# Order of the out products of the last two weight slabs of four two-stream layers (context first, latents after)

## What is computed

```python
def ffn_sublayer(x, shift, scale, gate, w_in, w_out, ln_g, ln_b):
    y = swiglu_2(modulate_2(x, shift, scale), w_in, w_out)
    return layer_norm(ALPHA * x + 0.5 * gate * y, ln_g, ln_b)
```

## Time and profile before

| | |
|---|---|
| median of 3 runs (lowest, highest) | 2701.93 us (2701.62, 2702.2) |
| the profiled execution, its time | 2698.95 us |
| its span, first to last instruction | 2697.1 us |
| its mean granted TensorE clock | 0.971 |
| TensorE matmul busy | 2531.8 us, 94% |
| VectorE busy | 1851.8 us, 69% |
| ScalarE busy | 1101.2 us, 41% |
| read from memory | 448.99 MB |

### The profile page before, as it was taken

One profiled execution on the slowest core, in us unless ns is written; L12 is line 12 of the kernel. 1 busy time (PEld: TensorE's weight loads), 2 busy tenths in 40 slices (PEclk: granted clock), 3 DMA queues, 4 the chain that ended last, 5 costly groups with the idle time before them and its releaser, 6 DMA issues.

```text
span 2697.1 us, 39723 instructions
## 1 busy us (share of the span) xinstructions
PE 2531.8 (94%) x15724; PEld 2282.1 (85%) x15724; DVE 1851.8 (69%) x3539; ACT 1101.2 (41%) x1631; POOL 0.2 (0%) x4
## 2 busy tenths in 40 slices
PE   4999989889989999899999899999899999798997
PEld 4998889789988888688888898888898888777997
DVE  7878977788879965535555569886584444575665
ACT  3444555344453323634222652222642222545443
POOL 0000000000000000000000000000000000000000
PEclk8999999989989999999999999999999999898999
DMA  8876846768767742422222266665273332312552
GB/s 310 299 247 201 269 160 232 263 228 288 246 197 251 221 138 68 146 94 86 86 91 90 86 189 206 191 196 195 87 269 122 94 101 76 92 57 74 186 185 96
DMA packets 161097, 452.65 MB, mean 168 GB/s; under 512 B 17680, under 2 KB 21264, under 8 KB 160912
## 3 DMA queue, kind: packets, MB, share of 16 engines
q1 hardware_dynamic: 160912, 450.11, 51.2%
HBM read 448.99 MB, written 1.05 MB: 167 GB/s over the span
## 4 chain that ended last, share of the span: by engine, by line
PE 58%; DVE 6%; ACT 4%; issue 1%; DMA 0%; SPq 0%; ACTq 0%; DVEq 0%
PE PS L985 18%; PE PS L986 18%; PE PS L987 18%; DVE wlo L1445 2%; ACT whi L1189 1%; PE PS L1006 1%; PE PS L1008 1%; DVE X L1534 1%; PE PS L1124 1%; DVE X L1532 1%; ACT NT L1242 1%; DVE RS L1501 1%; PE PS L1170 0%; DVE Ul L1538 0%; PE PS L1153 0%
## 5 line engine op out<-in xcount | busy, mean ns | idle before, releaser
L1445 DVE TENSOR_TENSOR wlo<-raw,whi 128x1024 fp32r<-128x1024 f32 x602 | 736.1, 1223 | 490.3 <-ACT whi L1189 487.6
L985 PE MATMUL PS<-Uh,wlo 128*128 128x256 f32 (+1 forms) x2992 | 972.8, 325 | 77.4 <-DVE Ul L1538 42.0
L986 PE MATMUL PS<-Ul,whi 128*128 128x256 f32 (+1 forms) x2992 | 954.3, 319 | 0.0
L987 PE MATMUL PS<-Uh,whi 128*128 128x256 f32 (+1 forms) x2992 | 954.2, 319 | 0.0
L1189 ACT ACTIVATE whi<-raw 128x1024 fp32r<-128x1024 f32 x602 | 632.7, 1055 | 718.7 <-PE PS L987 716.9
L985 PEld LDWEIGHTS PS<-Uh,wlo 128*128 128x128 f32 x2992 | 580.9, 194 | 131.3 <-issue 44.9
L986 PEld LDWEIGHTS PS<-Ul,whi 128*128 128x128 f32 x2992 | 583.5, 195 | 35.0 <-issue 0.2
L987 PEld LDWEIGHTS PS<-Uh,whi 128*128 128x128 f32 x2992 | 582.6, 195 | 34.9
L985 PE MATMUL PS<-Hh,wlo 128*128 128x256 f32 (+1 forms) x1616 | 529.5, 328 | 9.9 <-DVE X L1428 4.1
L986 PE MATMUL PS<-Hl,whi 128*128 128x256 f32 (+1 forms) x1616 | 514.1, 318 | 0.0
L987 PE MATMUL PS<-Hh,whi 128*128 128x256 f32 (+1 forms) x1616 | 513.9, 318 | 0.0
(11 more groups left out here) (170 smaller groups left out, 1918.9 us busy)
## 6 DMA issues: line engine op xcount, KB each, us to landing
MODS<-in_mm SPq DMA_DIRECT2D x168, 256.0 KB, 3.7
SCR<-in_mm SPq DMA_DIRECT2D x168, 256.0 KB, 3.7
raw<-in_f0i SPq DMA_DIRECT2D x64, 512.0 KB, 3.8
raw<-in_f1i SPq DMA_DIRECT2D x56, 512.0 KB, 3.5
raw<-in_f2i SPq DMA_DIRECT2D x56, 512.0 KB, 3.6
SCR<-in_ma SPq DMA_DIRECT2D x88, 256.0 KB, 5.0
raw<-in_w1i SPq DMA_DIRECT2D x44, 512.0 KB, 4.4
raw<-in_w2i SPq DMA_DIRECT2D x44, 512.0 KB, 4.3
```

The costliest lines, as they stand in the source:

```text
L985: e.matmul(o, ll, rh, start=start, stop=False)
L986: e.matmul(o, lh, rl, start=False, stop=False)
L987: return e.matmul(o, lh, rh, start=False, stop=stop)
L1445: e.tensor_tensor(wlo[:, w.n % RING, :], raw[:, w.n % RING, :], whi[:, w.n % RING, :].bitcast(F32), ALU.subtract).then_inc(s["wlo"].tell(w ...
```

## The change

The last slab but one of f0, go, f1 and f2 is no longer run for both streams at once. `outer_halves` is given the last two slabs. It runs the last but one for the context alone (by `outer`), then the last one for the context with squares and sums as before. The filler now holds two generators: the last slab's products for the latents, without squares and sums (its four pieces are still in the ring), and after them the last but one slab's products for the latents, now with squares and sums. These call `chunk` again, so the four pieces of that slab are fetched and split a second time, and `outer` got a parameter `every` so that it gives out one product at a time. The filler of the context's norm is thus sixteen products long instead of eight. On VectorE the order of the accumulations on a tile of X is no longer that of the slabs' numbers, so `x_before` now looks up which accumulation on that tile was the last.

```diff
-    def outer(self, st, w_out, first, slab, at, qs, r, norm=None):
+    def outer(self, st, w_out, first, slab, at, qs, r, norm=None, every=0):
...
             if mm % per == per - 1:
                 self.used[c] = (w.id, 0)
+            if every or mm % per == per - 1:
                 yield
...
-    def outer_halves(self, st, w_out, first, slab, at, qs, norm):
-        per, n0 = 8 // len(slab), len(self.stream)
-
-        def half(r):
+    def outer_halves(self, st, w_out, last_two, norm):
+        (first0, slab0, at0, qs0), (first, slab, at, qs) = last_two
+        per = 8 // len(slab)
+        self.drain(self.outer(st, w_out, first0, slab0, at0, qs0, CTX))
+        n0 = len(self.stream)
+
+        def kept(r):
             for mm in range(KT):
...
-                w = self.out_tile(st, n0 + c, slab, at, qs, mm, r, n0 + c, norm, True)
+                w = self.out_tile(st, n0 + c, slab, at, qs, mm, r, n0 + c, norm, r is CTX)
...
-        self.drain(half(CTX))
-        self.filler.append(half(LAT))
+        self.drain(kept(CTX))
+        self.filler.append(kept(LAT))
+        self.filler.append(self.outer(st, w_out, first0, slab0, at0, qs0, LAT, norm, 1))
...
-            if n:
+            if n and (r is not BOTH or n < len(slabs) - 1):
                 yield from out(n - 1)
...
-            self.outer_halves(st, w_out, firsts[n], slabs[n], n + at, [slots[f] for f in slabs[n]], norm)
+            self.outer_halves(st, w_out, [(firsts[i], slabs[i], i + at, [slots[f] for f in slabs[i]]) for i in (n - 1, n)], norm)
...
-        if n:
+        if 0 < n < len(CSLABS) - 1:
             p.drain(p.outer("go", "go", 4 * (n - 1), CSLABS[n - 1], n - 1, [((n - 1) % 2) * FS + i for i in range(FS)], BOTH))
-    n = len(CSLABS) - 1
-    p.outer_halves("go", "go", 4 * n, CSLABS[n], n, [(n % 2) * FS + i for i in range(FS)], True)
+    p.outer_halves("go", "go", [(4 * n, CSLABS[n], n, [(n % 2) * FS + i for i in range(FS)])
+                                for n in (len(CSLABS) - 2, len(CSLABS) - 1)], True)
...
-            def x_before(st, at, k, h):
-
-                if at and (st, at - 1, k, h) in s["acc"].at:
-                    on.wait_ge(s["acc"], (st, at - 1, k, h))
+            added = {}
+
+            def x_before(st, k, h):
+
+                if (st, k, h) in added:
+                    on.wait_ge(s["acc"], added[st, k, h])
                     return
...
+                    added[st, k, h] = (st, at, k, h)
```

More of the change, by code:

```diff
@@ L1426, in accumulate @@
                     on.wait_ge(s["coef"], (st, h))
-                    x_before(st, at, k, h)
+                    x_before(st, k, h)
                     e.scalar_tensor_tensor(out=X[:, k, l:u], in0=PS[:, bank[0], l:u], scalar=cf((st, h))[:, k:k + 1],
```

## The result

| | before | after |
|---|---|---|
| median (8 runs each, one chip) | 2701.78 us (2699.6 to 2702.84) | 2709.45 us (2707.1 to 2711.2) |
| the profiled execution, its span | 2698.95, 2697.1 us | 2707.65, 2705.9 us |
| mean granted clock | 0.971 | 0.969 |

The ratio is 1.0029 (95% interval 1.0019 to 1.0039): the kernel is slower by 7.7 us, where +9.2 was forecast.

The account below looks back on a forecast made before the run. TensorE, busy for 94% of the span, was taken to bound the kernel. Stage terms of 1.1 + 1.1 + 2.3 + 3.6 and 1.1 for f1's modulation work made +9.2 us on 2701.93, thus 2711, range 2698 to 2720.

Parts of the forecast that it names:

- Parts 1 and 2: Last slab but one as narrow products: 10.3 us less in its context pass, 11.5 more for latents; cost 1.25 per stage.
- Part 3: Sixteen more pieces of weights, four per stage, fetched and split again on ScalarE and VectorE: taken as costing nothing.
- Part 4: During the context's norm, waits for Ul go; TensorE idles 8.6 us for the re-fetched slab's first square, about the same size.
- The second wait of 1.6 us: TensorE waits 1.6 us more, for the square of the re-fetched slab's third latent product, which ends at 1925.3.
- Part 5: After the 8.6 us idle the clock is at 1.2 GHz: 1.0 us more per stage (ends 0 and 1.4).
- Part 6: Stage by stage, clock included: f0 +3.6, go +2.3, f1 and f2 +1.1 each, plus 1.1 for f1's modulation work.
- The clock's term: Low clock behind the long idle in each of the four stages: +1.0 us per stage.
- its first tile starts 0.4 us later after A; so +1.3: In go, the context norm's first tile starts 0.4 us later after the context's last sums: +1.3 us, with the clock +2.3.
- The lag: In f1, VectorE's modulation work falls behind the narrow products: ends 0 and 2.2 us, taken 1.1.
- The stall is really covered: Rival: squares ready when TensorE asks; 11 us less per stage in go, f1 and f2, nothing in f0; about 2669; 12%.
- It moves and costs little: Rival: clock returns at once, f1's VectorE keeps up, f0's latent tiles catch up; +3 us, 2705; 20%.
- The repeated weights come late: Rival: re-fetched pieces 2 to 4 each hold TensorE for a 2.3 us weights pass, 27 us in all, 2739; 8%.

Follow-up runs that it names:

- experiment 1: Kernel before, with the last slab but one as two narrow products per output tile, nothing moved or loaded twice: 2705.53 us, ratio 1.0020.
- experiment 2: Kernel before, with the last slab but one run for the context, then at once for the latents with weights fetched again: 2711.97 us, ratio 1.0041.
- experiment 3: Changed kernel, with two filler products instead of one after each tile of the context's norm: 2698.35 us, ratio 0.9992.
- experiment 5: Changed kernel, with the re-fetched slab's latent sums one product behind instead of two in f0, go and f1: 2714.36 us, ratio 1.0052.
- experiment 6: Changed kernel, with the re-fetched slab's latent sums three products behind instead of two in f0, go and f1: 2706.86 us, ratio 1.0022.
- experiment 11: Changed kernel, with three filler products per tile of the context's norm and f1's modulation work held back: 2694.01 us, ratio 0.9973.
- experiment 4: Changed kernel, with f0 left as in the kernel before: 2706.78 us, ratio 1.0023.

## Why the prediction came out as it did

**Parts 1 and 2 held.** -10.24 before A for -10.3, f1 apart. The cost of the width, 1.25, was measured alone as 1.03 to 1.32 per stage. The estimate from the Trainium skill's smaller figure would have made experiment 1 a change of 1 us; it was 4.9 ahead of A and 4.6 in the medians.

**Part 3 held, but for one stage.** The sixteen pieces cost nothing in f0, go and f2 (experiment 2). In f1 the loading of M beside modulation work isn't free.

**Part 4 held.** Its main figure was right to 0.1 us, for the reason given: the accumulation of M0 is queued behind tile 4's Ul. That it was so exact is luck in part: 1918.0 was got as 1.2 us before the last pair at its old time, while by the same text the pair itself moves to 1918.4. The accumulation starts 0.4 us before a pair, and the pair came where it was forecast (A + 23.7), so the two slips cancel. Experiments 3, 5, 6 and 11 move that wait from 9.97 down to 1.58 us by places in the order alone. The second wait of 1.6 us, for the square of M2, was nearly absent (0.11 us in f1). Work at half clock filled that time, so these two terms overlapped, and A to E came close to the 43.2 us that part 4 has without the clock.

**Part 5 was too large.** The clock was 0.50 for 10.2 us in f0, go and f2 and 6.8 in f1, beginning inside the long idle, as foretold. But its +1.0 per stage, added to part 4's times, was hardly there. The sums of M2 stand in part 4 at 1925.35, or A + 30.65, with the clock at full. They started at A + 30.77 in f0, 30.83 in go, 30.65 in f1 and 31.22 in f2: 0.9 us in all, for 4.0. TensorE in f1, the product that starts at A and the sums of M2:

```profile
1891.38 0.47 PE L993 MATMUL PS<-Hh,wlo 128*128 128x256 f32 x1
...
1922.03 0.70 PE L1014 MATMUL PS<-X,ones 128*128 128x256 f32 x2
```

Work slowed by the clock took the place of the wait of 1.6 us. What the clock would cost without the long wait is open: no experiment had the one without the other.

**Part 6.** The stages came out at 2.8, 0.8, 3.2 and 0.5 us for 3.6, 2.3, 2.2 and 1.1; the errors are -0.8, -1.5, +1.0 and -0.6, together -1.9 of 9.2. The clock's term was 0.4 to 1.0 us too large in each, and explains f0, which was right in sign and rank, and f2. In go a second step failed as well, "its first tile starts 0.4 us later after A; so +1.3": this difference of go from f1 was carried over, and it is gone. Its first tile now starts at A + 7.6 for A + 7.5 in f1, the wait for the square is the same 8.53 us, and A to E takes 43.0 us for 43.4. In f1 the clock's error is hidden by terms that were too small. The lag was forecast 1.1 and measured 2.0, still within the 0 to 2.2 given. The figures per piece were right (3.27 for 3.3), but behind the 0.4 x 4 us a 0.35 us wait already stood, and the cover I assumed for part of it wasn't there. And behind A TensorE has two waits that the prediction lacked, 0.43 us for the square of M4 and 0.4 more for wlo. So the 7.7 us lie nearer to the 9.2 than the single terms do.

**The rivals.** *The stall is really covered* fails with the 8.53 us. Its deciding point was M0's accumulation before 1910, or A + 15.3; it ran at 1914.71, or A + 23.3. But experiment 11 comes near to that case: with 1.58 us left it gains 7 us, not 33. Its price was also too high by its own part 4: 43.2 us less the waits of 8.6 and 1.6 is 33.0 us of work, not 31.5. The rival supposed that all 12 us of idling per stage could be filled; the accumulations and weights passes that come with the products which fill TensorE's time also stretch VectorE's chain behind them. *It moves and costs little* was too low for f1 and f0. *The repeated weights come late* was right nowhere as told, with no wait for wlo in M, but its engine, VectorE, was the one that made f1 late ahead of A.

## What to carry to other kernels

Filling an idle engine with work only helps if what the filler hands on to other in-order queues stands early enough there: look for the filler's own accumulations and squares in those queues, and work out where they start, before counting the idle time as won. A pass split in two has a price per instruction that the trace already shows, to be set against it (here 13 ns per pair, 5 us in all). And when work is added for cover, the rate at which it is given out has to be chosen anew: the same sixteen products cost 7.7 us at one per tile and gained 7.0 at three, with f1's modulation work held back; two per tile without the change lost 4.8.

## What was not expected of the hardware

A wait of 8.53 us, alike to 0.01 us in four stages of one execution, and steps of 1.44 and 1.45 us between experiments: where these two engines wait for each other, the trace repeats to 0.01 us, so such waits can be used as a ruler. Behind waits of 8.5 us and of 4.7 us the sums are slowed alike at first (a pair of them takes 1.22 and 1.06 us, for 0.70 at full clock), yet behind one of 1.58 us not at all (0.70 us): there the clock stayed at full, and the low stretch came some 18 us later, in the region of the short waits for Ul. The clock repeats less well than the waits. Behind the same wait of 2.50 us in f1 it stayed at 1.00 in two executions (the changed kernel, experiment 3) and fell to 0.50 for 3.4 us in three others (experiments 4, 5 and 6), which made 1.5 us of difference. And what a low stretch costs depends on what lies under it: the 6.8 us in f1 of the changed kernel had 2.9 us of work in them and cost nothing that can be seen at the sums of M2.
